# Leaving out the filler products on zeros in a two-layer attention, retention and gated-MLP trunk

## The chip, the cores and the metric

The kernel runs on one core of a Trainium2 chip. The metric is the device time of one execution in microseconds (us), the median of several runs. The engines are TensorE (PE in the profile, its weight loads PEld), VectorE (DVE), ScalarE (ACT), GpSimd (POOL) and SyncE (SP, which issues the transfers of the weights).

## What is computed

256 tokens of width 1024 pass through two layers. The reference, cut to what matters:

```python
def reference(x, p, positions, w_in, ...):
    for i in range(DEPTH):                                   # DEPTH = 2
        mix = token_mixer(x, positions, w_in[i], ...)
        x = layer_norm(DN_ALPHA * x + mix, ln1_g[i], ln1_b[i])
        ple = jax.nn.sigmoid(x @ w_ple_gate[i]) * (p[i] @ w_ple_proj[i])
        x = layer_norm(DN_ALPHA * x + conv_ffn(x, w_up[i], conv_w[i], conv_b[i], w_down[i]) + ple,
                       ln2_g[i], ln2_b[i])
    return x
```

`token_mixer` projects x onto q, k, v and gates of three dilated attention groups (8 heads) and of a retention mixer (4 heads), and merges both through projections. All operands are float32.

## The kernel before

**Products.** Each float32 product is made of three products of parts: an operand is split into a high and a low part, and `split_product` (L921) issues high by high, high by low and low by high (L923, L924, L925). The transposed activations stand in `xT_hi` and `xT_lo`, 256 tokens wide, in two tiles t of 128 tokens.

**Weights.** All weights go through one ring of three slots, in chunks of 1 MB. SyncE loads a chunk into `raw`, ScalarE rounds it into `w_hi` (L304), VectorE subtracts to get `w_lo` (L527; at three places a layer GpSimd does it, L869). `weights_ready` (L927) makes TensorE wait for a chunk's `w_lo`. One chunk against the tokens is 48 products with 256 columns: `by_token` (L942) has the tokens as the stationary operand and waits for each token tile's `xT_lo` before that tile's half, `transposed` (L930) has the weights as the stationary operand.

**A layer.** The order on each engine is written out by hand. TensorE runs four turns of 15 chunks with attention and retention between them, then the merge (gates, projections, `w_out` into the four accumulators `acc`), then the two products of the per-layer embedding (`ple`), then four chunks of `w_ple_gate` by `by_token`, then the MLP (eleven times two chunks of `w_up` and one of `w_down`).

**The two LayerNorms.** The first one (here LN1) comes after the last `w_out` chunk, the second (LN2) after the last `w_down` chunk. VectorE adds the residual to each accumulator (L542), takes the statistics (L545, L552), GpSimd makes the reciprocal root (L874), VectorE writes the normalised rows `Y` (L560, semaphore `ln_y`). TensorE transposes them by eight transposes for each token tile (`transpose_y`, L981, instructions at L984). VectorE (L587) and ScalarE (L319) apply gain and bias to four blocks each into `xT_f`, ScalarE rounds to `xT_hi` (L326), VectorE subtracts to `xT_lo` (L579). Only then can the first product of the next stage start. VectorE's order is: `Y` of tile 0, statistics of tile 1, `xT_f` of tile 0, `Y` of tile 1, `xT_lo` of tile 0, `xT_f` and `xT_lo` of tile 1. At LN1 the products of `ple` stand between the last accumulation and the transposes of tile 1; at LN2 nothing does. LN2 of the last layer needs no transposes.

**The filler products.** `keep_clock(n)` (L959) issues n products of the all-zero tile `zero_r` into `bank[0]`, 128 by 128 against 512 columns each. Nothing reads what they write, since the next real product on that bank starts afresh. They stand at four places of the code: 10 before the loop over the layers; in each layer 2 before and 8 after the transposes of tile 1 of LN1; and, in the first layer alone, 7 before the transposes of tile 0 of LN2 and 14 between those of tile 0 and of tile 1.

Of the kernel before, what the change touches and what calls it, by code (L numbers as in the profile page):

```python
# [91 lines left out]
def program(nc, x, xT, positions, w_in, w_attn_proj, w_ret_proj, w_out, w_up, w_down,  # L92
            w_ple_gate, ple_operands, ln_rows, feature_params, constants, out):
    ctx = ExitStack()
    with ctx:
# [822 lines left out]
        def _(pe):  # L918
# [40 lines left out]
            def keep_clock(n):  # L959

                for _ in range(n):
                    mm(bank[0][:, :], zero_r[:, 0:P], zero_r[:, :], start=True, stop=True)
# [18 lines left out]
            def transpose_y(n, t):  # L981
                pe.wait_ge(ln_y, n * TT + t + 1)
                for k in range(KT):
                    ins = nc.tensor.transpose(acc[2 * t + k // 4][:, (k % 4) * P:(k % 4 + 1) * P],  # L984
                                              Y[:, t, k * P:(k + 1) * P], ident)
                    if k % 4 == 3:
                        ins.then_inc(lnT_done, 1)
# [2 lines left out]
            pe.wait_ge(zeros_set, 1)  # L990
            pe.wait_ge(xT_hi_ready, 1)
            pe.wait_ge(bank_read[0], 1)
            keep_clock(10)
            with pe.Fori(0, DEPTH) as l:
                with pe.Fori(0, NJ) as j:
                    it = pe.snap(l * NJ + j)
# [126 lines left out]
                            transpose_y(l * 2, 0)  # L1123
                    ins.then_inc(chunk_done, 1)
                pe.wait_ge(bank_read[0], l * USES[0] + (U_PLE[0] + 2))
                keep_clock(2)
                transpose_y(l * 2, 1)
                keep_clock(8)
                for j in range(NJ):
                    pe.wait_ge(bank_read[j], l * USES[j] + (U_PLE[j] + 2))  # L1130
                    by_token(c0, 2 + j, j, l * 2 + 1 if j == 0 else None)
# [17 lines left out]
                from_mid(c0, -1, l * (NJ + NF) + (NJ + NF), slot=1, last=True)  # L1149
                with pe.If(DEPTH - 1 - l):  # L1150
                    pe.wait_ge(bank_read[0], l * USES[0] + (USES[0] + 1))
                    keep_clock(7)
                    transpose_y(l * 2 + 1, 0)
                    keep_clock(14)
                    transpose_y(l * 2 + 1, 1)


# [55 lines left out]
```

## Time and profile before

| | |
|---|---|
| median of 3 runs | 1589.49 us (1587.81 to 1591.19) |
| span of the profiled execution, first to last instruction | 1586.6 us |
| TensorE busy | 1543.5 us, 97% |
| VectorE busy | 947.0 us, 60% |
| ScalarE busy | 753.7 us, 48% |
| GpSimd busy | 81.3 us, 5% |
| mean granted TensorE clock | 0.990 |

The rows come from one profiled execution. Its span of 1586.6 us is the time that is given for it; the median lies 2.9 us above it. The granted clock is a share of full speed: 1.00 is 2.4 GHz and 0.50 is 1.2 GHz, and a value between them in a stretch is a mixture of the two. In a timeline the first number is the start in us, the second the duration, and the brackets hold the idle time before and what ended it. TensorE's durations overlap, so the spacing of starts tells the pace.

### The profile page before, as it was taken

Reading aid. Unit: us, or ns where it says so; the run is one execution under the profiler, and the core shown is the slowest. Engines: PE = TensorE matmul, PEld = TensorE weight load, DVE = VectorE, ACT = ScalarE, POOL = GpSimd, SP = SyncE. Lnnn points to the kernel's source line nnn. Section 1 sums busy time; section 2 is a strip of 40 time slices with the busy share of each in tenths; the row PEclk is TensorE's granted clock in tenths of the full one; section 3 lists DMA queues with packets and bytes.
Section 4 is the critical chain, followed back from the end, with each engine's and each line's share of the span. In section 5 each row is a group of like instructions: output and inputs, shape, how many; then the busy total and the mean of one; then the engine's idle time right before and its main releaser. Section 6 shows DMA issues by size and latency. Waiting matters only on the chain.

```text
span 1586.6 us, 28993 instructions
## 1 busy us (share of the span) xinstructions
PE 1543.5 (97%) x11795; PEld 1494.1 (94%) x11795; DVE 947.0 (60%) x1013; ACT 753.7 (48%) x806; POOL 81.3 (5%) x45
## 2 busy tenths in 40 slices
PE   7999999999999999999989999999999999899995
PEld 7999999999999989999789999999999999899995
DVE  5644655546544587666756456455464545876666
ACT  5445354454533356555444544544444334465652
POOL 0000000000000041000210000000000001400001
PEclk9999999999999999999989999999999999999998
DMA  9545544444455546556445364453545555555550
GB/s 301 180 135 175 167 134 160 157 159 160 155 190 184 173 159 213 172 185 198 133 151 174 106 210 135 157 177 114 187 157 172 181 178 173 184 184 185 188 185 27
DMA packets 233205, 266.35 MB, mean 168 GB/s; under 512 B 4160, under 2 KB 223808, under 8 KB 232640
## 3 DMA queue, kind: packets, MB, share of 16 engines
q1 hardware_dynamic: 230688, 258.56, 49.4%
q10 hardware_dynamic: 2464, 7.06, 1.2%
q8 instruction: 36, 0.59, 0.2%
q14 instruction: 17, 0.14, 0.0%
HBM read 264.55 MB, written 1.05 MB: 167 GB/s over the span
## 4 chain that ended last, share of the span: by engine, by line
PE 81%; issue 14%; DVE 3%; ACT 1%; DMA 1%; POOL 0%; SPq 0%; DVEq 0%; ACTq 0%; POOLq 0%
PE bank L923 23%; PE bank L924 23%; PE bank L925 23%; PE acc L923 2%; PE acc L924 2%; PE acc L925 2%; PE acc L1020 1%; PE acc L1006 1%; PE acc L1015 1%; DVE xT_lo L579 1%; PE acc L1003 1%; PE acc L1022 1%; DMA raw<-w_in 1%; PE acc L1070 0%; PE acc L1042 0%
## 5 line engine op out<-in xcount | busy, mean ns | idle before, releaser
L527 DVE TENSOR_TENSOR w_lo<-raw,w_hi 128x2048 fp32r<-128x2048 f32 x240 | 559.7, 2333 | 411.7 <-ACT w_hi L304 411.0
L923 PE MATMUL bank<-xT_hi,w_hi 128*128 128x256 f32 x2240 | 636.9, 284 | 0.0
L925 PE MATMUL bank<-xT_hi,w_lo 128*128 128x256 f32 x2240 | 634.5, 283 | 0.0
L924 PE MATMUL bank<-xT_lo,w_hi 128*128 128x256 f32 x2240 | 634.4, 283 | 0.0
L304 ACT ACTIVATE w_hi<-raw 128x2048 fp32r<-128x2048 f32 x246 | 469.4, 1910 | 166.7 <-PE bank L925 94.3
L923 PEld LDWEIGHTS bank<-xT_hi,w_hi 128*128 128x128 f32 x2240 | 430.0, 192 | 1.9 <-DVE w_lo L527 0.4
L924 PEld LDWEIGHTS bank<-xT_lo,w_hi 128*128 128x128 f32 x2240 | 430.1, 192 | 1.5
L925 PEld LDWEIGHTS bank<-xT_hi,w_lo 128*128 128x128 f32 x2240 | 430.1, 192 | 0.0
L923 PE MATMUL bank<-w_hi,xT_hi 128*128 128x256 f32 x768 | 222.5, 290 | 7.3 <-DVE xT_lo L579 6.5
L312 ACT ACTIVATE scratch<-bank 128x512 f32<-128x512 f32 x112 | 67.0, 598 | 332.6 <-PE bank L925 332.5
L924 PE MATMUL bank<-w_lo,xT_hi 128*128 128x256 f32 x768 | 218.8, 285 | 0.0
L925 PE MATMUL bank<-w_hi,xT_lo 128*128 128x256 f32 x768 | 218.5, 285 | 0.0
L923 PEld LDWEIGHTS bank<-w_hi,xT_hi 128*128 128x128 f32 x768 | 148.7, 194 | 10.8 <-DVE xT_lo L579 8.7
L924 PEld LDWEIGHTS bank<-w_lo,xT_hi 128*128 128x128 f32 x768 | 148.8, 194 | 0.2
L925 PEld LDWEIGHTS bank<-w_hi,xT_lo 128*128 128x128 f32 x768 | 148.7, 194 | 0.0
L813 DVE SCALAR_TENSOR_TENSOR scratch<-scratch,feat 128x256 f32<-128x256 f32 x176 | 77.6, 482 | 66.5 <-ACT scratch L484 60.6
L923 PE MATMUL acc<-w_hi,mid_hi 128*128 128x512 f32 x240 | 94.0, 392 | 0.9 <-DVE mid_lo L532 0.9
L924 PE MATMUL acc<-w_lo,mid_hi 128*128 128x512 f32 x240 | 93.8, 391 | 0.0
L925 PE MATMUL acc<-w_hi,mid_lo 128*128 128x512 f32 x240 | 93.5, 389 | 0.0
L925 PE MATMUL bank<-ret_hi,w_lo 128*128 128x256 f32 x256 | 72.5, 283 | 0.0
L924 PE MATMUL bank<-ret_lo,w_hi 128*128 128x256 f32 x256 | 72.5, 283 | 0.0
L923 PE MATMUL bank<-ret_hi,w_hi 128*128 128x256 f32 x256 | 72.5, 283 | 0.0
(156 smaller groups left out, 1478.6 us busy)
## 6 DMA issues: line engine op xcount, KB each, us to landing
raw<-w_in SPq DMA_DIRECT2D x136, 1024.0 KB, 5.0
raw<-w_up SPq DMA_DIRECT2D x44, 1024.0 KB, 5.1
raw<-w_down SPq DMA_DIRECT2D x22, 1024.0 KB, 4.8
raw<-w_ret_proj SPq DMA_DIRECT2D x16, 1024.0 KB, 5.0
raw<-w_attn_proj SPq DMA_DIRECT2D x8, 1024.0 KB, 4.9
raw<-w_out SPq DMA_DIRECT2D x8, 1024.0 KB, 5.1
raw<-w_ple_gate SPq DMA_DIRECT2D x8, 1024.0 KB, 4.9
scratch<-ln_rows ACTq DMA_DIRECT2D x4, 1024.0 KB, 5.6
```

The lines of the kernel that those rows point to most:

```text
L304: nc.scalar.activation(w_hi[:, s, :], raw[:, s, :], ACT.Copy).then_inc(hi_ready, 1)
L312: nc.scalar.activation(dst, src, func, scale=scale).then_inc(bank_read[b], 1)
L527: nc.vector.tensor_tensor(w_lo[:, s, :], raw[:, s, :], w_hi[:, s, :].bitcast(F32), ALU.subtract).then_inc(lo_ready, 1)
L579: nc.vector.tensor_tensor(xT_lo[v], xT_f[v], xT_hi[v].bitcast(F32), ALU.subtract)\
L813: ins = nc.vector.scalar_tensor_tensor(out=conv[:, 2 * half + b, :], in0=hpad[:, 2 * half + b, tap:tap + SEQ], scalar=feat[:, bass.ds(i * ...
L923: mm(dst, st_hi, mv_hi, start=start, stop=False)
L924: mm(dst, st_hi, mv_lo, start=False, stop=False)
L925: return mm(dst, st_lo, mv_hi, start=False, stop=stop)
L1003: mm(acc[0][:, g * P:(g + 1) * P], qk[:, 2 * g, a, 0:P], qk[:, 2 * g + 1, a, 0:P], start=True, stop=True)
L1006: ins = mm(acc[1 + g // 2][:, (g % 2) * SEQ:(g % 2 + 1) * SEQ], qk[:, 2 * g, a, P:SEQ], qk[:, 2 * g + 1, a, :], start=True, stop=True)
L1015: ins = nc.tensor.transpose(acc[g][:, o * P:(o + 1) * P], prob[:, src:src + P], ident)
L1020: mm(acc[a][:, 0:SEQ], att_v[:, g, 0, a * P:(a + 1) * P], probT[:, a, g, 0:SEQ], start=(g == 0), stop=False)
```

## The change

All five calls of `keep_clock` are removed. The function itself, `zero_r` and every wait stay as they were.

```diff
--- before.py
+++ after.py
@@ -990,7 +990,6 @@
             pe.wait_ge(zeros_set, 1)
             pe.wait_ge(xT_hi_ready, 1)
             pe.wait_ge(bank_read[0], 1)
-            keep_clock(10)
             with pe.Fori(0, DEPTH) as l:
                 with pe.Fori(0, NJ) as j:
                     it = pe.snap(l * NJ + j)
@@ -1123,9 +1122,7 @@
                             transpose_y(l * 2, 0)
                     ins.then_inc(chunk_done, 1)
                 pe.wait_ge(bank_read[0], l * USES[0] + (U_PLE[0] + 2))
-                keep_clock(2)
                 transpose_y(l * 2, 1)
-                keep_clock(8)
                 for j in range(NJ):
                     pe.wait_ge(bank_read[j], l * USES[j] + (U_PLE[j] + 2))
                     by_token(c0, 2 + j, j, l * 2 + 1 if j == 0 else None)
@@ -1149,9 +1146,7 @@
                 from_mid(c0, -1, l * (NJ + NF) + (NJ + NF), slot=1, last=True)
                 with pe.If(DEPTH - 1 - l):
                     pe.wait_ge(bank_read[0], l * USES[0] + (USES[0] + 1))
-                    keep_clock(7)
                     transpose_y(l * 2 + 1, 0)
-                    keep_clock(14)
                     transpose_y(l * 2 + 1, 1)
```

## Rows read from the trace of the kernel before

**Rows 1.** The page: share of each engine, and the chain that ended last.

```profile
PE 1543.5 (97%) x11795; PEld 1494.1 (94%) x11795; DVE 947.0 (60%) x1013; ACT 753.7 (48%) x806; POOL 81.3 (5%) x45
...
PE 81%; issue 14%; DVE 3%; ACT 1%; DMA 1%; POOL 0%; SPq 0%; DVEq 0%; ACTq 0%; POOLq 0%
```

**Rows 2.** TensorE's waits: us in total, times, longest.

```profile
PE acc L984 <- DVE scratch L560: 9.7, 3, 3.3
PE bank L923 <- DVE xT_lo L579: 6.5, 3, 5.2
```

**Rows 3.** Groups by line, shapes apart: the filler products.

```profile
L962 PE MATMUL bank<-zero_r 128*128 128x512 f32 x51 | 18.4, 518 | 9.8 <-ACT xT_hi L338 9.8
```

**Rows 4.** Timeline of TensorE at the start of the kernel.

```profile
9.78 4.60 PE L962 MATMUL bank<-zero_r 128*128 128x512 f32 x10 [9.78 <-ACT xT_hi L338]
14.67 0.58 PE L923 MATMUL bank<-w_hi,xT_hi 128*128 128x256 f32 x1 [0.29 <-DVE w_lo L527]
...
15.47 0.41 PE L923 MATMUL bank<-w_hi,xT_hi 128*128 128x256 f32 x1
15.69 0.41 PE L924 MATMUL bank<-w_lo,xT_hi 128*128 128x256 f32 x1
...
16.40 0.28 PE L923 MATMUL bank<-w_hi,xT_hi 128*128 128x256 f32 x1
16.52 0.28 PE L924 MATMUL bank<-w_lo,xT_hi 128*128 128x256 f32 x1
```

**Rows 5.** Busy time by stretch, LN1 of layer 0; PEclk is the granted clock.

```profile
564.00:568.00 4.00, 1.77 (x9) 1.78 (x10) 4.00 (x2) 0.64 (x2) 4.00 (x2) 0.69 0.33 88
568.00:572.00 4.00, 3.83 (x10) 2.53 (x10) 4.00 (x4) 1.50 (x4) 3.09 (x2) 0.50 0.50 174
572.00:576.00 4.00, 4.00 (x32) 3.91 (x33) 2.29 (x6) 2.97 (x4) 0.00 (x0) 0.96 0.00 0
```

**Rows 6.** Timeline of TensorE, LN1 of layer 0.

```profile
566.23 1.97 PE L984 MATMUL acc<-const,scratch 128*128 128x128 f32 x8 [3.29 <-DVE scratch L560]
...
567.84 3.76 PE L962 MATMUL bank<-zero_r 128*128 128x512 f32 x8
...
571.77 0.58 PE L923 MATMUL bank<-w_hi,xT_hi 128*128 128x256 f32 x1 [0.17 <-DVE xT_lo L579]
```

**Rows 7.** Timeline of TensorE, LN1 of layer 1.

```profile
1352.84 1.09 PE L984 MATMUL acc<-const,scratch 128*128 128x128 f32 x8 [3.28 <-DVE scratch L560]
...
1353.69 3.52 PE L962 MATMUL bank<-zero_r 128*128 128x512 f32 x8
...
1358.39 0.39 PE L923 MATMUL bank<-w_hi,xT_hi 128*128 128x256 f32 x1 [1.18 <-DVE xT_lo L579]
...
1364.98 0.39 PE L923 MATMUL bank<-w_hi,xT_hi 128*128 128x256 f32 x1 [0.19 <-DVE w_lo L527]
```

**Rows 8.** Busy time by stretch, LN1 of layer 1.

```profile
1352.00:1356.00 4.00, 3.16 (x14) 2.71 (x15) 4.00 (x3) 1.50 (x4) 3.92 (x3) 0.75 0.68 227
1356.00:1360.00 4.00, 2.82 (x16) 2.00 (x16) 3.61 (x5) 0.35 (x1) 1.79 (x1) 0.83 0.11 36
```

**Rows 9.** Timeline of TensorE, LN2 of layer 0.

```profile
786.86 3.43 PE L962 MATMUL bank<-zero_r 128*128 128x512 f32 x14
793.39 1.25 PE L984 MATMUL acc<-const,scratch 128*128 128x128 f32 x8 [3.10 <-DVE scratch L560]
799.83 0.57 PE L923 MATMUL bank<-w_hi,xT_hi 128*128 128x256 f32 x1 [5.19 <-DVE xT_lo L579]
...
804.26 0.36 PE L925 MATMUL bank<-w_hi,xT_lo 128*128 128x256 f32 x1
```

**Rows 10.** Busy time by stretch, LN2 of layer 0.

```profile
791.00:795.00 4.00, 1.25 (x8) 0.86 (x8) 4.00 (x2) 0.33 (x1) 4.00 (x2) 0.90 0.13 44
...
803.00:807.00 4.00, 4.00 (x30) 4.00 (x30) 1.46 (x2) 3.20 (x2) 2.05 (x2) 0.82 0.13 37
```

**Rows 11.** Timeline of VectorE, LN2 of layer 0.

```profile
793.25 5.58 DVE L579 TENSOR_TENSOR xT_lo<-scratch,xT_hi 128x512 fp32r<-128x512 f32 x2
```

## The prediction

> **What bounds the kernel now.** I read the page first, then TensorE's waits, then the four places of the fillers in the timeline, and last the granted clock around them. The page says that TensorE is busy for 97% of the span and is 81% of the chain that ended last [rows 1]. VectorE and ScalarE have slack nearly everywhere, so what makes TensorE slower makes the kernel longer by as much, unless the same stretch holds a wait that something else ends. The list of waits shows where that is so: TensorE waits three times for the normalised rows (9.7 us) and three times for `xT_lo` (6.5 us), at the three LayerNorms that are followed by more work [rows 2]. The fillers run inside those waits and at the start. They are 51 products with 18.4 us of busy time [rows 3], 1.2% of the span, and the question is whether a single one of them is on the path, and what the clock does without them.
>
> At each place something other than the fillers ends the wait. At the start the ten fillers run from 9.78 to 14.38, and then TensorE still waits 0.29 us for the first `w_lo` [rows 4]. At LN1 of layer 0 an idle time of 3.29 us stands between the two fillers and the transposes, and after the eight fillers another of 0.17 us, ended by `xT_lo` [rows 6]; in layer 1 the same two are 3.28 and 1.18 us [rows 7]. At LN2 the fourteen fillers end at 790.29, and idle times of 3.10 and 5.19 us follow [rows 9]. So their 18.4 us free nothing by themselves.
>
> **What they do for the clock now.** At the start, the real products come every 0.21 us (15.47, 15.69) and soon after every 0.12 us (16.40, 16.52): six of them, from 14.67 until about 15.9, ran at the slow pace [rows 4]. The granted clock cannot be read there, since these first stretches have no record of a change; the spacing is the evidence. At LN1 of layer 0 the clock is 0.69 over 564 to 568, which is 2.5 us at half and puts the fall at 565.5; 0.96 over 572 to 576 is 0.3 us more, so it rises at 572.3, 0.5 us after the first real product [rows 5, 6]. At LN1 of layer 1, 0.75 and 0.83 make it low from 1354.0 to 1357.4, and the first real product at 1358.39 finds 2.4 GHz [rows 7, 8]. At LN2, 0.90 and 0.82 make it low from 794.2 to 804.4, and the products from 799.83 to 804.26, 21 of them, run at 1.2 GHz all the same: there the fillers end too early to help [rows 9, 10].
>
> **The price of a cold start.** A product with 256 columns costs 0.214 us at 1.2 GHz and 0.12 us at 2.4 GHz, so a microsecond of cold work loses 1 - 0.12/0.214 = 0.44 us. How long TensorE must work before the clock is back is shown four times: 4.6 us at LN2, with nothing but real products; 3.7 us at LN1 of layer 1 and 4.5 us at LN1 of layer 0, each from the first filler after the transposes; 6.1 us at the start, from 9.78 to 15.9 [rows 4 to 10]. I take 4.6 us, the one that consists of real products and lies near the middle, hence a loss of 2.0 us for each cold start, and keep 3.7 us (1.6 us lost) and 6.1 us (2.7 us lost) for the range.
>
> The Trainium skill, "TensorE: Matmul & The Clock Gate", section "Terms", puts the penalty at the throttled time times one minus the ratio of the clocks, that is one half; by it the loss would be 2.3 us instead of 2.0 for the same cold stretch. The measured spacing of 0.12 us, above half of 0.214, decides for me. The same page's section "Why this matters for your kernels" speaks against this change: it asks for short pauses between bursts of products, lest the clock fall; the pause at LN2, where it did fall, agrees.
>
> **Part by part.**
>
> *Start, 10 fillers.* Removed, TensorE stands idle until 14.67, and the first product starts then as before, because it waits for `w_lo`. It starts cold: 2.0 us lost, where now 6 products times 0.094 = 0.55 us are lost. Net +1.5 us (1.1 to 2.2). Nothing later gives it back: from there TensorE is the bound, with no wait in its list until the merge.
>
> *LN1, 2 and 8 fillers in each layer.* Without them TensorE is idle from about 562 to 571.8, but for the transposes. The clock must be low when the first product starts, since two pauses of 3.9 and 3.5 us or more stand there, and at LN2 pauses of 3.10 and 5.19 us left it low. The transposes may run at half clock. That costs nothing: they took 1.97 us in layer 0 and 1.09 in layer 1, and the first product came 5.54 and 5.55 us after their start [rows 6, 7], because VectorE's chain (`Y` of tile 1, `xT_lo` of tile 0) sets it. The cold start loses 2.0 us, but part is covered: between the first product at 1358.39 and the next chunk at 1364.98, which waits for its `w_lo`, lie 6.59 us, and 48 products at 0.12 us need only 5.76 [rows 7]. `w_lo` there follows VectorE's and ScalarE's work on tile 1, not TensorE's products, so 0.83 us are hidden. That same cover hides the 0.5 cold us of layer 0 now. Net 2.0 - 0.83 = +1.2 us in each layer (0.8 to 1.9), +2.4 us for both. If the cover were gone it would be 4.0 less the 0.25 lost now.
>
> *LN2, 7 and 14 fillers in layer 0.* The stage starts cold with them and without them: 2.0 us lost both times, net 0. The length of the cold stretch may come out otherwise, -0.4 to +0.7 us. The transposes of tile 1 may be up to 0.9 us slower, and VectorE takes their result only after `xT_lo` of tile 0 at 798.83 [rows 11], over 3 us after they end. One thing the trace leaves open: the first product starts 1.0 us after that `xT_lo`, where at LN1 it starts within 0.1 us. TensorE goes back to the head of the loop there, and something in its own instruction stream holds it. Fewer instructions might take that microsecond away or add another: 1.0 us either way, and I take none.
>
> The sum is 1.5 + 2.4 + 0 = +3.9 us on the span: 1586.6 + 3.9 = 1590.5 us, and with the 2.9 us by which the median stands above the span, 1593.4 us (+0.25%). A measurement of this kernel can tell about 0.2%, 3.2 us, from no change. The low ends make 1.1 + 1.6 - 0.4 - 1.0 = +1.3 us, the high ends 2.2 + 3.8 + 0.7 + 1.0 = +7.7 us, which are 1590.8 and 1597.2 us. The runs before lie from 1.7 below to 1.7 above their median, so I widen it a little, mostly below.
>
> **Rivals.**
>
> *Slower by 2.2 to 3.1 us: the cover takes most of it (not slower).* If the clock returns after about 3.7 us as at LN1 of layer 1, the terms are 1.1, 0.8 and 0.8, and LN2 gains 0.4: +2.3 us, 1591.8 us, inside the 0.2%. It decides below a cold stretch of 4.2 us. For it speaks that one of four stretches was so short; against it that the other three are 4.5 to 6.1 us. Two of the four began on fillers and hold a wait, so neither is quite what a cold start of real products would be. Chance 0.26.
>
> *The fillers hold back what they wait for (faster).* A filler that is still in the queue when the awaited tile is there delays the real work. The place is LN2, where the seven fillers end about when `Y` of tile 0 is ready, and the 1.0 us before the first product; at LN1 of layer 0 the last filler ends 0.17 us ahead of it. At most that is 1.0 us at LN2 and 0.2 elsewhere, 1.2 us gained, and it would need cold starts that cost nothing: 1588.3 us. It decides only if the path held more than 3.2 us of filler time; the idle times behind every group of fillers speak against it. Chance 0.04.
>
> *A longer cold stretch (slower by more).* If each cold start lasts 6.1 us as at the start of the kernel, or if the clock falls again during the stage because products waiting for weights leave gaps: 2.2 + 3.8 + 0.7 = +6.7 us, 1596.2 us. For it speaks the start, the only place where TensorE came from a long idle time; against it LN2, where the products alone had the clock back in 4.6 us. Chance 0.15.
>
> *The change does nothing.* If the clock kept its level through the pauses without fillers, only the start would change. The fall at LN2 amid idle time speaks against it; it would be about +1.5 us at most, 1591.0 us. Chance 0.05.
>
> The forecast itself, +3.2 to +5.5 us, has 0.50. Slower by over 0.2% is the forecast and the longer stretch, less a little for scatter of the median across the bound: 0.64; within 0.2% is 0.32; faster 0.04. The range of 1589.9 to 1597.5 us leaves out less than 2 in 10.
>
> **What would show it.** In the profile after, L962 is gone and TensorE's idle time grows by about 18 us, at the same places. The first product still starts at about 14.7 after `w_lo`, and some 17 to 29 products follow at a spacing of 0.21 us, at the start, at both LN1 and at LN2. The granted clock at both LN1 stays 0.50 for several us past the first product, and TensorE's wait of 0.19 us for `w_lo` in `w_ple_gate`'s second chunk is gone. The distance from the last accumulation to the first product is the same at LN1. I am wrong if real products after LN1 start at 2.4 GHz, if the first product of a stage moves by more than a few tenths, or if the clock falls in places with no LayerNorm.

## The result and the profile after

The changed kernel takes 1592.4 us (median of 10 runs, 1591.31 to 1593.17), the kernel before 1588.77 us (median of 10). The ratio is 1.0023, 95% interval 1.0014 to 1.0032: slower by 3.6 us, with an interval of 2.2 to 5.1 us. The forecast was 3.9 us slower and 1593.4 us. The kernel before has a median here 0.7 us below the 1589.49 us of its first three runs, so the forecast's absolute time lies 1.0 us off and its difference 0.3 us.

The page of the changed kernel has the same picture as [rows 1], with a longer span and 11.6 us less busy time on TensorE. The fillers had 18.4 us, but the products that now run at 1.2 GHz are busy for longer, and some of the fillers' recorded time overlapped with that of the transposes:

```profile
span 1589.8 us, 28891 instructions
PE 1531.9 (96%) x11744; PEld 1487.2 (94%) x11744; DVE 946.4 (60%) x1013; ACT 754.2 (47%) x806; POOL 81.1 (5%) x45
```

TensorE's waits after, against [rows 2]:

```profile
PE acc L984 <- DVE scratch L560: 15.1, 4, 6.3
PE bank L923 <- DVE w_lo L527: 14.6, 1, 14.6
PE bank L923 <- DVE xT_lo L579: 11.9, 3, 4.3
```

TensorE's idle time (the span less its busy time) grew from 43.1 to 57.9 us, by 14.8 us, at the places where the fillers stood; the forecast had about 18. The 14.6 us are the wait for the very first product, of which 9.8 and 0.3 us stood there before. The short waits for `w_lo` behind both LN1 are gone from the list, as are the products of [rows 3].

The timeline of TensorE after, at the start, at LN1 of layer 0, at LN2 and at LN1 of layer 1, four views that answer to [rows 4, 6, 7, 9]. First the start:

```profile
14.56 0.58 PE L923 MATMUL bank<-w_hi,xT_hi 128*128 128x256 f32 x1 [14.56 <-DVE w_lo L527]
...
20.05 0.41 PE L924 MATMUL bank<-w_lo,xT_hi 128*128 128x256 f32 x1
20.27 0.41 PE L925 MATMUL bank<-w_hi,xT_lo 128*128 128x256 f32 x1
...
20.64 0.28 PE L924 MATMUL bank<-w_lo,xT_hi 128*128 128x256 f32 x1
20.76 0.28 PE L925 MATMUL bank<-w_hi,xT_lo 128*128 128x256 f32 x1
```

The first product starts 0.1 us from its old place, and the products come every 0.21 us until 20.5, where before they did so until 15.9. Then LN1 of layer 0:

```profile
568.15 1.97 PE L984 MATMUL acc<-const,scratch 128*128 128x128 f32 x8 [3.72 <-DVE scratch L560]
573.66 0.58 PE L923 MATMUL bank<-w_hi,xT_hi 128*128 128x256 f32 x1 [3.54 <-DVE xT_lo L579]
```

LN2:

```profile
795.81 1.97 PE L984 MATMUL acc<-const,scratch 128*128 128x128 f32 x8 [6.31 <-DVE scratch L560]
802.11 0.58 PE L923 MATMUL bank<-w_hi,xT_hi 128*128 128x256 f32 x1 [4.33 <-DVE xT_lo L579]
```

LN1 of layer 1:

```profile
1354.64 1.50 PE L984 MATMUL acc<-const,scratch 128*128 128x128 f32 x8 [3.74 <-DVE scratch L560]
1360.14 0.58 PE L923 MATMUL bank<-w_hi,xT_hi 128*128 128x256 f32 x1 [4.00 <-DVE xT_lo L579]
```

From the transposes to the first product it is 5.51, 6.30 and 5.50 us; before it was 5.54, 6.44 and 5.55 us. So the fillers held back at most 0.05 us at an LN1. At LN2, counted from the start of the last `w_down` chunk, the transposes of tile 0 come 0.14 us sooner without the seven fillers ahead of them (7.07 against 7.21 us), and those of tile 1 only 0.05 us sooner. The slower transposes cost nothing. What changed is the clock that the products find. Busy time by stretch after, at LN1 of both layers (the number behind the five engines is the granted clock), against [rows 5, 8]:

```profile
572.00:576.00 4.00, 2.34 (x11) 2.34 (x12) 3.30 (x6) 1.08 (x3) 1.06 (x1) 0.50 0.00 0
576.00:580.00 4.00, 4.00 (x32) 4.00 (x32) 2.97 (x3) 3.68 (x3) 0.00 (x0) 0.88 0.00 0
...
1364.00:1368.00 4.00, 4.00 (x30) 4.00 (x30) 3.58 (x3) 2.15 (x2) 0.00 (x0) 0.82 0.03 5
```

(Over 1360 to 1364 the clock is 0.50 too.) A clock of 0.88 over 576 to 580 is 1.0 us at half, so it rose at 577.0, 3.3 us after the first product of layer 0; 0.82 over 1364 to 1368 puts the rise at 1365.4, 5.3 us after the first product of layer 1. At LN2 the same reading gives 805.6, 3.5 us after it.

From these starts the 3.2 us between the two spans can be laid out by place. The start of the kernel to the first product after LN1 of layer 0: 573.66 against 571.77, +1.9 us. On to the first product after LN2: 228.45 against 228.06, +0.4. On to LN1 of layer 1: 558.03 against 558.56, -0.5. On to the end: 229.7 against 228.2, +1.5 us. The second and the fourth hold what LN1 costs, the third what LN2 does. A second profile of the same kernel (`e9_after_again` below) gives +0.7, +1.4, 0.0 and +1.8 us for the four, so a single part can be off by about 1 us from one execution to the next. The two agree that both LN1 cost something and that LN2 costs nothing.

### The profile page after: what moved, and what is told of

Its sections match the earlier page's. It is cut to its first block, busy times and chain, and to the rows that moved or that the text cites. A ratio compares the mean times of both kernels' runs of the same rounds, so it can differ in the third digit from the quotient of the medians.

```text
span 1589.8 us, 28891 instructions
## 1 busy us (share of the span) xinstructions
PE 1531.9 (96%) x11744; PEld 1487.2 (94%) x11744; DVE 946.4 (60%) x1013; ACT 754.2 (47%) x806; POOL 81.1 (5%) x45
## 4 chain that ended last, share of the span: by engine, by line
PE 82%; issue 14%; DVE 2%; ACT 0%; DMA 0%; POOL 0%; ACTq 0%; DVEq 0%; SPq 0%; POOLq 0%
PE bank L923 23%; PE bank L924 23%; PE bank L925 23%; PE acc L923 2%; PE acc L924 2%; PE acc L925 2%; PE acc L1019 1%; PE acc L1005 1%; PE acc L1014 1%; DVE xT_lo L579 1%; PE acc L1002 1%; PE acc L1021 1%; PE acc L1069 0%; PE acc L1041 0%; DMA scratch<-xT 0%
## 5 line engine op out<-in xcount | busy, mean ns | idle before, releaser
L923 PE MATMUL bank<-w_hi,xT_hi 128*128 128x256 f32 x768 | 224.3, 292 | 26.4 <-DVE w_lo L527 14.6
L923 PEld LDWEIGHTS bank<-w_hi,xT_hi 128*128 128x128 f32 x768 | 151.1, 197 | 27.8 <-issue 14.6
```

The lines of the kernel that those rows point to most:

```text
L923: mm(dst, st_hi, mv_hi, start=start, stop=False)
```

## The experiments

Each ratio is to the kernel before, timed beside the run on the same chip. `e4_covered` and `e6_start40` have 4 runs, the others 9 to 11.

**One place at a time.** The three parts of the change were taken alone.

`e1_start_only`:

```diff
-            keep_clock(10)
```

> Only the 10 fillers at the start are left out. Cold-start theory: the first real product still starts at about 14.6 us and 17 to 29 products run at 1.2 GHz before the clock is back; the kernel becomes 1.1 to 2.2 us longer (+0.07 to +0.14%), and both LN1 and LN2 look as before. Rival, fillers hold back what they wait for: the first product starts earlier and the kernel is not slower. Rival, the longer cold stretch: over 2.2 us slower, with slow products in later stages too.

Measured: ratio 1.0009, interval 1.0000 to 1.0018, that is +1.4 us. In its profile the first product starts at 14.32 and the clock rises at 18.2, a cold stretch of 3.9 us. Both LN1 start at full clock, and after LN2 the first 2.8 us are cold, against 4.6 us in the kernel before. The forecast's size stands, at the edge of what can be told from nothing: the interval is 0 to 2.9 us.

`e2_ln1_only`:

```diff
-                keep_clock(2)
                 transpose_y(l * 2, 1)
-                keep_clock(8)
```

> Only the 2 and the 8 fillers at LN1 are left out, in both layers. Cold-start theory: after each LN1 the first 17 to 29 products run at 1.2 GHz, less 0.83 us of cover by the wait for the next chunk's w_lo: 0.8 to 1.9 us in each layer, 1.6 to 3.8 us in all (+0.10 to +0.24%), and the wait of 0.19 us for w_lo is gone. Rival, the cover takes most of it: under 1.6 us. Rival, the change does nothing there: the products after LN1 start at 2.4 GHz, 0 us.

Measured: ratio 1.0013, interval 1.0004 to 1.0022, +2.1 us. The cold stretches in its profile are 3.7 us after LN1 of layer 0 and 5.5 us after that of layer 1. The rival by which the clock keeps its level is out. The cover is real too: the wait for `w_lo` behind each LN1 is gone, as in the changed kernel.

`e3_ln2_only`:

```diff
-                    keep_clock(7)
                     transpose_y(l * 2 + 1, 0)
-                    keep_clock(14)
```

> Only the 7 and the 14 fillers at LN2 of layer 0 are left out. Cold-start theory: the stage starts cold with and without them, so the time stays within -0.4 and +0.7 us, and the first product comes about 1 us after xT_lo as before. Rival, the fillers hold back the loop's restart: that gap of 1.0 us closes to 0.1 us and the kernel is 1 us faster. Rival, they keep part of the clock: the cold stretch after LN2 grows to 6 us, +0.7 us.

Measured: ratio 0.9998, interval 0.9989 to 1.0007: no difference. These 21 fillers, two fifths of all, bought nothing. The gap between `xT_lo` and the first product did not close either (`xT_lo` ends at 798.6, the product starts at 799.71), so it isn't the fillers that hold the loop's restart. The three ratios add up to +0.20%, and the whole change is +0.23%.

The profile of this run showed something else, at LN1 of layer 1, where it has all of its fillers. TensorE there:

```profile
1353.83 2.09 PE L962 MATMUL bank<-zero_r 128*128 128x512 f32 x8
1358.52 0.58 PE L923 MATMUL bank<-w_hi,xT_hi 128*128 128x256 f32 x1 [2.60 <-DVE xT_lo L579]
```

and the granted clock:

```profile
1356.00:1360.00 4.00, 1.48 (x7) 1.48 (x8) 3.75 (x5) 0.22 (x1) 1.92 (x1) 0.73 0.14 43
```

In this execution the clock was still up after the transposes. So the eight fillers took 2.09 us instead of the 3.52 of [rows 7], ended 2.60 us ahead of the first product, and the clock fell in that gap, at 1357.9. The products then ran at 1.2 GHz for 6.2 us. A fixed number of fillers protects less when it starts warm. It is no single case: five of the profiles (the kernel before, `e1_start_only`, this run, `e6_start40` and `e7_start40_looped`) have the eight fillers behind both LN1, and in three of these ten places the fillers took only 2.09 to 2.10 us and the products behind them were cold, for 6.2 us here, 6.2 us in `e7_start40_looped` in layer 0 and 3.3 us in `e6_start40` in layer 1.

**More fillers instead of none.** If the clock is the mechanism, filling the waits entirely must remove the cold stretches that the kernel before has.

`e4_covered`:

```diff
-            pe.wait_ge(xT_hi_ready, 1)
             pe.wait_ge(bank_read[0], 1)
-            keep_clock(10)
+            keep_clock(40)
...
-                keep_clock(2)
+                keep_clock(16)
                 transpose_y(l * 2, 1)
-                keep_clock(8)
+                keep_clock(18)
...
-                    keep_clock(7)
+                    keep_clock(6)
                     transpose_y(l * 2 + 1, 0)
-                    keep_clock(14)
+                    keep_clock(27)
                     transpose_y(l * 2 + 1, 1)
+                    keep_clock(18)
```

> More fillers instead of none: 40 from about 2 us on at the start (the wait for xT_hi ahead of them is dropped), 16 and 18 at LN1, 6 and 27 at LN2 and 18 more behind its last transposes, so that every wait is filled with them at full clock. Cold-start theory: no real product runs at 1.2 GHz at the start, after LN1 or after LN2; against before that saves 2.0 us at LN2 and 0.3 to 0.55 at the start, 2.3 to 2.6 us faster (-0.15%). Rival, fillers hold back what they wait for: the first products of the stages start later than before by the overrun, and the kernel is not faster.

Measured: ratio 1.0119, interval 1.0102 to 1.0135, 19 us slower. Neither expectation held. Every stage began at full clock, and at LN1 the first products came 5.6 us after the transposes, where before it was 5.5. After LN2 the clock fell all the same, 0.3 us behind the first product and for 3.4 us, after TensorE had stood idle for 1.99 us ahead of it; it also fell at two turns of the mixer loop. And TensorE's list of waits has a new head, with "issue" for time in which the engine waited for nothing that the profile shows:

```profile
PE bank L923 <- issue: 16.9, 7, 2.6
```

Six of these seven stand at the turns of the mixer loop, where nothing had stood before, and the seventh after LN2; one of the six in the timeline:

```profile
324.12 0.38 PE L923 MATMUL bank<-w_hi,xT_hi 128*128 128x256 f32 x1 [2.55 <-issue]
```

The list of transfer queues shows 91 packets in the queue of instructions q8:

```profile
q8 instruction: 91, 1.49, 0.4%
```

where the page of the kernel before has 36 packets and 0.59 MB for that queue. So a new theory is that TensorE fetches its code again at each turn, and the next runs test it.

**What made the code be fetched again.**

`e5_waits_only` keeps the many fillers in the layers and takes the start of the kernel before:

```diff
+            pe.wait_ge(xT_hi_ready, 1)
             pe.wait_ge(bank_read[0], 1)
-            keep_clock(40)
+            keep_clock(10)
```

> As e4_covered (16 and 18 fillers at LN1, 6 and 27 and 18 at LN2), but with the start as in the kernel before, 10 fillers behind the wait for xT_hi. Theory A, e4_covered lost its time because 30 more fillers ahead of the loops moved TensorE's code and each turn of the mixer loop now fetches instructions again: here the six idle times of about 2.4 us at the loop's turns are gone, the instruction queue has about 36 packets again instead of 91, and the kernel is 0.7 to 2 us faster than before. Theory B, the fillers inside the layers cause them: they stay, and so do some 15 us.

Measured: ratio 0.9997, interval 0.9988 to 1.0006. The instruction queue is back at 36 packets and the six idle times are gone, as theory A has it. Against before the gain of 0.7 to 2 us did not show beyond the noise: the median is 0.5 us lower. The granted clock never fell from the start to the end of the last stage:

```profile
core 0: 1585.6 us, clock 0.996
```

Only the final LayerNorm, with no product behind it, is left at half clock. So the cold products are gone. In the profile of the kernel before they were 5.9 us at the start and after LN2, which at 0.44 would make a gain of 2.6 us; the interval reaches only to 1.9 us. One part of the difference is lost at LN2:

```profile
793.77 1.09 PE L984 MATMUL acc<-const,scratch 128*128 128x128 f32 x8 [0.27 <-DVE scratch L560]
794.61 4.36 PE L962 MATMUL bank<-zero_r 128*128 128x512 f32 x18
800.69 0.38 PE L923 MATMUL bank<-w_hi,xT_hi 128*128 128x256 f32 x1 [1.72 <-issue]
```

The first product comes 6.92 us after the transposes instead of 6.44 [rows 9], and the wait before it is no longer put down to `xT_lo` but to "issue".

`e6_start40` and `e7_start40_looped` have the 40 fillers at the start and else the kernel before. In the first they stand in the code forty times, in the second ten times in a loop:

```diff
-            pe.wait_ge(xT_hi_ready, 1)
             pe.wait_ge(bank_read[0], 1)
-            keep_clock(10)
+            keep_clock(40)                    # e6
+            with pe.Fori(0, 4) as _:          # e7
+                keep_clock(10)
```

> The kernel before, only with 40 fillers at the start from about 2 us on instead of 10. Theory A: the six idle times of 2.3 to 2.6 us at the turns of the mixer loop appear, with some 90 packets of instructions, and the kernel is 14 to 19 us slower although the clock is up at the first real product. Theory B: no such idle times, and the kernel is 0.3 to 0.5 us faster.

> The same 40 fillers at the start as e6_start40, but written as a loop of four times ten, so that TensorE's code is as long as before. Theory A, the length of the code matters and not the work: no idle times at the mixer loop's turns, about 36 packets of instructions, 0.3 to 0.5 us faster than before. If the 40 products themselves did it, 14 to 19 us slower as e6_start40.

Measured: `e6_start40` 1.0134 (1.0118 to 1.0149), 21 us slower, with 90 packets of instructions and 14.8 us of "issue" in six waits of at most 2.6 us:

```profile
q8 instruction: 9, 0.15, 0.7%
```

The line is the instruction queue of `e6_start40` over 118 to 221 us, the second turn of the mixer loop: nine packets of 16 KB. The third turn has nine more. From 101 to 417 us, in which the second and third turns and most of the fourth lie, it is 27 packets, and the kernel before has none there after 104 us. The second layer has about as many again, and the two pages differ by 54. Only TensorE's code was changed, and it is fetched again at each turn.

`e7_start40_looped` 0.9998 (0.9989 to 1.0007), with 36 packets and none of those waits. The same work in shorter code costs nothing, so the code ahead of the mixer loop is the cause and the 40 products are not. Whether it is its length or where it leaves the loop's own code, the runs don't tell apart. The loss is more than the 14.8 us of waits. Three cold stretches that the profile of the kernel before does not have lie in it: 3.4 us at each of two turns, and 3.3 us after LN1 of layer 1. At 0.44 they make 4.4 us, 0.8 of it covered; with the waits that is 18.4 of the 19.1 us between the two profiled spans. The hoped-for 0.3 to 0.5 us of `e7_start40_looped` are below what the runs can show. In its profile the fillers ended at 13.0, 2.0 us before the first product, and the clock fell at 16.0, 1.0 us behind the first product: again a number of fillers that did not reach.

`e8_covered_looped` is `e4_covered` with the start of `e7_start40_looped` and 12 instead of 18 fillers behind the last transposes of LN2.

```diff
-            keep_clock(40)
+            with pe.Fori(0, 4) as _:
+                keep_clock(10)
...
                     transpose_y(l * 2 + 1, 1)
-                    keep_clock(18)
+                    keep_clock(12)
```

> All waits covered with the 40 fillers at the start in a loop, and 12 instead of 18 behind LN2's last transposes, since in e4_covered the first product after them started 7.2 us after the transposes where before it is 6.4. Cold-start theory: no real product at 1.2 GHz, LN2 starts at most 0.5 us later, 1.5 to 2.3 us faster than before (about -0.12%). Rival, the fillers behind the transposes hold the loop's restart by as much as the clock gives: 0 to -0.5 us.

Measured: ratio 1.0005, interval 0.9996 to 1.0014. No gain, so the expectation of 1.5 to 2.3 us failed. In the profile, the twelve fillers ended 3.4 us before the first product and the clock fell at 799.6, 0.4 us before it, so that 3.0 us were cold. Fewer fillers did not bring that product forward either: it came 7.2 us after the transposes, as in `e4_covered`.

**The changed kernel once more, and LN2 left bare.**

`e9_after_again` is the changed kernel.

> The changed kernel once more. Cold-start theory: the median is again 3.2 to 4.5 us above before (+0.2 to +0.28%); in its profile all four stages (start, LN1 twice, LN2) begin at 1.2 GHz, but the four cold stretches have other lengths than in the first profile (6.0, 3.3, 3.5, 5.3 us), anywhere from 2.8 to 6.2 us, since they do not depend on the code. If they do depend on it, the same four lengths come back.

Measured: ratio 1.0027, interval 1.0017 to 1.0037. Its cold stretches are 3.8 us at the start, 5.4 and 5.9 us after the two LN1, and 4.7 us after LN2, where the first profile had 6.0, 3.3, 5.3 and 3.5 us. Same code, other lengths.

`e10_ln2_tail_bare` is `e5_waits_only` without the fillers behind the last transposes:

```diff
                     transpose_y(l * 2 + 1, 1)
-                    keep_clock(18)
```

> As e5_waits_only, without the 18 fillers behind the last transposes of LN2, so only LN1 and the start are covered. Cold-start theory: the stage after LN2 starts 0.5 us sooner after its transposes than in e5 (6.4 against 6.9 us) but with 2.8 to 6 us at 1.2 GHz, so 0.7 to 2.2 us slower than e5_waits_only; against before 0 to 0.9 us faster, since LN1 never starts cold. Rival, the fillers behind the transposes cost as much as they give: the same time as e5.

Measured: ratio 1.0002, interval 0.9993 to 1.0011. The first product after LN2 starts 5.97 us after the transposes and is cold for 5.8 us. It cannot be told from `e5_waits_only` by time (both intervals hold 1 and overlap), so whether the 18 fillers there pay stays open.

The cold stretch behind the first product of each stage, from the granted clock of the profiles (us; 0 where the product found full clock), for the kernels whose code isn't fetched again at the mixer loop's turns:

| kernel | start | LN1, layer 0 | LN2 | LN1, layer 1 |
|---|---|---|---|---|
| before | 1.3 | 0.5 | 4.6 | 0 |
| after | 6.0 | 3.3 | 3.5 | 5.3 |
| after, again | 3.8 | 5.4 | 4.7 | 5.9 |
| start bare | 3.9 | 0 | 2.8 | 0 |
| LN1 bare | 0.7 | 3.7 | 3.9 | 5.5 |
| LN2 bare | 0 | 0 | 5.2 | 6.2 |
| LN1 and LN2 filled (`e5`) | 0 | 0 | 0 | 0 |
| 40 in a loop at the start (`e7`) | 3.4, from 1.0 us on | 6.2 | 5.0 | 0 |
| all filled, start in a loop (`e8`) | 0 | 0 | 3.0 | 0 |
| LN1 filled, LN2's tail bare (`e10`) | 0 | 0 | 5.8 | 0 |

## Why the prediction was right

**The fillers free nothing.** Right. The first products start as far behind the transposes as before, within 0.05 us at LN1 and 0.14 us at LN2, and TensorE's idle time grew by more than its busy time fell.

**The price of a cold start.** I took 4.6 us cold and 2.0 us lost, with 3.7 to 6.1 us for the range. The eight cold stretches in the two profiles of the changed kernel run from 3.3 to 6.0 us, with a mean of 4.7 us. That the mean is so close to the 4.6 us is partly luck, since that figure was one reading and the prediction took it for what TensorE must work before the clock is back. It is no fixed amount: the same code gave 6.0 and 3.8 us at the start. The spacing of 0.21 and 0.12 us stood as read, and with it the 0.44. The Trainium skill ("TensorE: Matmul & The Clock Gate", section "Terms") puts the loss at the throttled time times one minus the ratio of the clocks, which is one half. The spacing here does not agree with it, and the time cannot tell the two apart, since half of each cold stretch would make some 4.6 us in all (an estimate with that page's half and the prediction's other terms) and the interval is 2.2 to 5.1 us.

**Start, +1.5 us.** The stretch measured +1.9 and +0.7 us in the two profiles and the part alone +1.4 us (interval 0 to 2.9). Right in size, as far as that tells it from nothing.

**LN1, +1.2 us in each layer.** In the first profile +0.4 (with a cold stretch of 3.3 us, and a gap at LN2 that was 0.1 us shorter) and +1.5 us (5.3 us cold); the part alone +2.1 us for both. The cover of 0.83 us fits both: 0.44 times 3.28 is 1.44, less 0.83 is 0.6; 0.44 times 5.28 is 2.32, less 0.83 is 1.5 us. It fits the second profile as well, where 5.4 and 5.9 us make 1.6 and 1.8 us, and +1.4 and +1.8 us were measured. What I left out is that the kernel before isn't safe at LN1 either. It had 0.5 and 0 us of cold work in the execution that I read, but the same fillers let 6.2, 6.2 and 3.3 us through at three of the ten LN1 in the profiles that have them. Beyond the cover that is some 0.4 us for each LN1 on the mean, an estimate from 0.44 times these stretches less 0.83. The prediction put this at nothing, so its 2.4 us for both is too high by about 0.9 us on the mean over executions. The measured +2.1 us has an interval of 0.6 to 3.5 us and cannot show it.

**LN2, 0.** Right: -0.5 us in the first profile, where the cold stretch was 1.1 us shorter, 0.0 in the second, where it was 4.7 us, and no difference in the part alone. The 1.0 us that I left open there is not made by the fillers.

**The rivals.** The longer cold stretch happened in single places (6.0 us at the start, 5.9 us after one LN1), never at all four in one execution. The cover took 0.8 us of each and not most, and the mean stretch of 4.7 us lies above the 4.2 us below which that rival decides; by time alone its 2.2 to 3.1 us are not ruled out, since they lie inside the interval. The fillers hold back at most 0.05 us where they stand now. Where some were put behind LN2's transposes, the first product came 6.9 to 7.2 us after these (three profiles), against 6.0 to 6.6 us in the nine others. That the clock keeps its level through the pauses is ruled out by the cold stretches behind both LN1 in all three profiles without the fillers there. The chance of 0.32 for a change within 0.2% was not too high: the measured 0.23% lies just outside, and its interval reaches inside.

## What to carry to other kernels

Judge filler products by the clock that the first real products find behind them and not by their busy time: here 21 of the 51 did nothing, since the wait went on for several us after them. A count that is right for a cold engine is too short for a warm one, so size it by the full clock where the clock is sure to be up, and read several executions. Even with every product of the layers at full clock (`e5_waits_only`) no gain over the 51 fillers could be told from nothing. And count the code: here thirty more straight-line fillers ahead of a long loop cost 19 to 21 us, where at most some 0.6 us was to be had at that place, while the same fillers in a small loop cost nothing.

## What was not expected

Thirty more products in the code ahead of the mixer loop made TensorE wait 2.3 to 2.6 us at six turns of that loop (the second to the fourth in each layer), with 90 instead of 36 packets in the instruction queue and 19 to 21 us in all. Between the last transposes of LN2 and the first product of layer 1, a turn of the outer loop takes 6.0 to 7.2 us, although `xT_lo` is there 0.5 to 1.7 us sooner. The instruction queue says more. In the kernel before, a packet of code starts at 796.51, ahead of the product at 799.83, and is the only one from 796 to 798:

```profile
q8 instruction: 1, 0.02, 3.2%
```

In all twelve profiles such a packet starts 3.1 to 3.4 us ahead of that product. It comes 2.8 to 3.3 us after the transposes' start, and 3.6 to 3.9 us after it in the three with fillers behind the transposes. That fits a turn that waits for its code, as at the turns of the mixer loop in `e6_start40`; no run took this packet away, so it isn't shown. Last, the cold stretches of one and the same code differ by up to 2.2 us between two executions (6.0 and 3.8 us at the start).
